# The mixer's output projection as seven quarter products, in a one-core encoder layer on Trainium2

## The reference, cut to what matters

```python
def hybrid_mixer(x, w_in, ..., w_out):
    ...
    return jnp.concatenate([att, hm.reshape(B, S, ML_WIDTH)], axis=-1) @ w_out

def memory_cross_attention(x, mem, w_cq, w_ck, w_cv, w_co):
    q = (x @ w_cq).reshape(B, S, MEM_HEADS, MEM_HD)
    k = (mem @ w_ck).reshape(B, -1, MEM_HEADS, MEM_HD)
    v = (mem @ w_cv).reshape(B, -1, MEM_HEADS, MEM_HD)
    ...

def reference(x, mem, ...):
    mix = hybrid_mixer(h, ...)
    h = layer_norm(DEEPNORM_ALPHA * h + mix, ln1_g[l], ln1_b[l])
    ca = memory_cross_attention(h, mem, ...)
    h = layer_norm(DEEPNORM_ALPHA * h + ca, ln2_g[l], ln2_b[l])
    ff = moe_ffn(h, ...)          # 32 experts, w_gu and w_down
    h = layer_norm(DEEPNORM_ALPHA * h + ff, ln3_g[l], ln3_b[l])
```

## Time and profile before

| | |
|---|---|
| median of 3 runs | 1160.19 us (1160.15 to 1160.58) |
| the profiled execution: its time | 1160.38 us |
| its span (first to last instruction) | 1158.4 us |
| mean granted TensorE clock over the span | 0.965 |
| busy: PE, DVE, ACT, POOL | 92%, 33%, 15%, 6% |
| HBM read | 443.84 MB |

### The profile page before, as it was taken

One profiled execution on the slowest core, in us unless ns is written; L12 is line 12 of the kernel. 1 busy time (PEld: TensorE's weight loads), 2 busy tenths in 40 slices (PEclk: granted clock), 3 DMA queues, 4 the chain that ended last, 5 costly groups with the idle time before them and its releaser, 6 DMA issues.

```text
span 1158.4 us, 20097 instructions
## 1 busy us (share of the span) xinstructions
PE 1070.6 (92%) x8036; PEld 469.1 (40%) x8037; DVE 378.1 (33%) x1230; ACT 168.5 (15%) x380; POOL 64.8 (6%) x40
## 2 busy tenths in 40 slices
PE   9999999998999669999976669999989989998997
PEld 8668649653333213333322223333323333332333
DVE  1716545254333113333311113333323313332323
ACT  1123211211111001111100001111111111111112
POOL 0520451000000000000000000000000000000000
PEclk9999999999999979999998889999998999999999
DMA  9984246959999999999999999999999999999996
GB/s 329 374 287 146 74 145 255 409 198 411 427 435 432 431 431 431 429 434 432 432 431 431 433 429 434 432 431 432 430 432 431 433 430 428 432 429 432 430 423 250
DMA packets 36670, 445.33 MB, mean 384 GB/s; under 512 B 3936, under 2 KB 5216, under 8 KB 21696
## 3 DMA queue, kind: packets, MB, share of 16 engines
q1 hardware_dynamic: 33888, 439.85, 90.3%
q10 hardware_dynamic: 2752, 5.04, 1.3%
HBM read 443.84 MB, written 1.05 MB: 384 GB/s over the span
## 4 chain that ended last, share of the span: by engine, by line
PE 72%; DMA 23%; another core or an unknown queue 2%; DVE 2%; ACT 1%; issue 0%; SPq 0%; DVEq 0%
PE bank L923 23%; PE bank L948 13%; DMA ring<-in_w_down 11%; DMA ring<-in_w_gu 11%; PE bank L899 6%; PE bank L600 6%; PE bank L617 5%; PE bank L886 3%; PE bank L819 2%; PE bank L756 2%; PE bank L698 2%; PE bank L892 1%; PE bank L930 1%; PE bank L936 1%; PE bank L941 1%
## 5 line engine op out<-in xcount | busy, mean ns | idle before, releaser
L923 PE MATMUL bank<-ring,wk 128*32 128x512 f32 x3072 | 371.1, 634 | 64.7 <-DMA ring<-in_w_gu 64.7
L923 PEld LDWEIGHTS bank<-ring,wk 128*32 128x32 f32 x3072 | 103.9, 116 | 304.2 <-issue 266.4
L948 PE MATMUL bank<-ring,wk 128*32 128x512 f32 x1632 | 205.5, 601 | 7.4 <-DMA ring<-in_w_down 7.3
L1829 DVE TENSOR_SCALAR wk<-bank 128x256 f32<-128x256 f32 x51 | 21.6, 424 | 536.1 <-PE bank L923 536.1
L899 PE MATMUL bank<-wk 64*128 64x512 f32 x416 | 103.3, 615 | 2.9 <-ACT wk L1329 2.9
L948 PEld LDWEIGHTS bank<-ring,wk 128*32 128x32 f32 x1632 | 63.4, 110 | 76.9 <-issue 48.9
L1315 ACT ACTIVATE wk<-wk 128x256 f32<-128x256 f32 x51 | 21.2, 416 | 455.2 <-DVE wk L1829 455.2
L600 PE MATMUL bank<-ring 128*128 128x256 f32 x320 | 70.4, 380 | 0.0
L899 PEld LDWEIGHTS bank<-wk 64*128 64x128 f32 x416 | 35.8, 186 | 71.5 <-issue 64.1
L600 PEld LDWEIGHTS bank<-ring 128*128 128x128 f32 x320 | 60.3, 190 | 8.4 <-issue 0.3
L886 PE MATMUL bank<-res,wk 128*32 128x256 f32 x832 | 56.5, 389 | 0.0
(11 more groups left out here) (333 smaller groups left out, 860.7 us busy)
## 6 DMA issues: line engine op xcount, KB each, us to landing
ring<-in_w_gu SPq DMA_DIRECT2D x55, 4096.0 KB, 34.7
ring<-in_w_down SPq DMA_DIRECT2D x27, 4096.0 KB, 38.3
ring<-in_w_gu SPq DMA_DIRECT2D x18, 2048.0 KB, 14.5
ring<-in_w_down SPq DMA_DIRECT2D x9, 2048.0 KB, 11.9
ring<-in_w_in SPq DMA_DIRECT2D x4, 2048.0 KB, 24.5
ring<-in_w_ck SPq DMA_DIRECT2D x2, 2048.0 KB, 22.0
ring<-in_w_cv SPq DMA_DIRECT2D x2, 2048.0 KB, 13.8
ring<-in_w_out SPq DMA_DIRECT2D x2, 2048.0 KB, 15.2
```

The source lines that it names most:

```text
L923: ins = mm(hidden(bank, g), rows[:, kk, c, :], half_columns(w[:, kk, :], g), start=False, stop=2 * c + kk == KT - 1, skip_group_check=True)
L948: ins = mm(strip(7, 2 * d + b), actT[:, b, 2 * c + gg, :], wd[:, gg, b, 512 * d:512 * d + 512], start=c == 0 and gg == 0 and b == 1, stop= ...
```

## The change

It does six things.

1. `wo0` and `wo1` become seven quarter products into banks 4, 5 and 6 (X, Y, Z), four matmuls each. Three of them add to a bank in place. They wait on `wo_sums` (input sums ready) and `wo_added` (a bank has been read).
2. DVE makes the sums: `wo_t1` and `wo_t3` before the copy of `hmT`; `wo_s1` to `wo_s4`, `wo_t2` and `wo_t4` between the products. Three of the weight sums are written over quarters of the weights.
3. DVE adds the products to `res` as they come: seven additions in place of four, each with one PSUM bank, and takes the statistics in halves between them.
4. `cq_t1` and `cq_t3` move on DVE from before the projection to between the projection's fifth and sixth product's additions.
5. POOL's sums for `cv` start on `wo_sums` 3 in place of `mixer_done`.
6. `wo_t1` uses the place of `lnp`, so the load of the first LayerNorm's parameters (ACT's queue) is issued after the fourth product; both `wo` slots are released to SP after the seventh.

```diff
@@ SP
             elif piece == "co0":
                 eng.wait_ge(co_half, 1)
+            elif piece in ("wo0", "wo1"):
+                eng.wait_ge(wo_product, 7)
@@ POOL
-            pool.wait_ge(mixer_done, 1)
+            pool.wait_ge(wo_sums, 3)
             pool.wait_ge(memT_landed, 16)
@@ PE
-            project("wo0", tT, order=(4, 5, 6, 7, 0, 1, 2, 3), late="pv")
-            project("wo1", tT)
+            landed("wo0")
+            landed("wo1")
+            X, Y, Z = psum[4], psum[5], psum[6]
+            quarter_product(X, mixed[0][0], wo_quarter[0][0]).then_inc(wo_product, 1)
+            wait_taken(pe, "pv")
+            quarter_product(Y, mixed[0][1], wo_quarter[1][0]).then_inc(wo_product, 1)
+            pe.wait_ge(wo_sums, 1)
+            quarter_product(Z, wo_s1, wo_t1).then_inc(wo_product, 1)
+            pe.wait_ge(wo_sums, 2)
+            pe.wait_ge(wo_added, 1)
+            quarter_product(X, wo_s2, wo_t2, fresh=False).then_inc(wo_product, 1)
+            pe.wait_ge(wo_sums, 3)
+            pe.wait_ge(wo_added, 3)
+            quarter_product(Z, wo_s4, wo_quarter[1][1], fresh=False).then_inc(wo_product, 1)
+            pe.wait_ge(wo_added, 4)
+            quarter_product(X, wo_s3, wo_t3, fresh=False).then_inc(wo_product, 1)
+            pe.wait_ge(wo_sums, 4)
+            quarter_product(Y, mixed[1][1], wo_t4).then_inc(wo_product, 1)
@@ ACT
-            act_e.dma_start(lnp, ln_p[0:1].to_broadcast([P, 2 * D])).then_inc(ln_landed[0], 16)
...
+            act_e.wait_ge(wo_product, 4)
+            act_e.dma_start(lnp, ln_p[0:1].to_broadcast([P, 2 * D])).then_inc(ln_landed[0], 16)
             rstd(0, 0)
@@ DVE, before the copy of hmT
+            link(v.tensor_tensor(wo_t1, wo_quarter[0][1], wo_quarter[0][0], ALU.subtract))
+            v.tensor_tensor(wo_t3, wo_quarter[1][1], wo_quarter[0][1], ALU.subtract)
@@ DVE, after it
+            v.tensor_tensor(wo_s1, mixed[1][0], mixed[1][1], ALU.add).then_inc(wo_sums, 1)
+            dve.wait_ge(wo_sums, 1)
+            v.tensor_tensor(wo_s2, wo_s1, mixed[0][0], ALU.subtract)
+            dve.wait_ge(wo_product, 1)
+            add_to_residual(0, 0, X).then_inc(wo_added, 1)
+            v.tensor_tensor(wo_t2, wo_quarter[1][1], wo_t1, ALU.subtract).then_inc(wo_sums, 1)
+            dve.wait_ge(wo_sums, 2)
+            v.tensor_tensor(wo_s4, mixed[0][1], wo_s2, ALU.subtract)
+            v.tensor_tensor(wo_s3, mixed[0][0], mixed[1][0], ALU.subtract).then_inc(wo_sums, 1)
...
```

More of the change, by code:

```diff
@@ L174, in layer_program @@
         queries = [[cqT[:, 4 - 4 * i:8 - 4 * i, t * P:t * P + P] for i in range(2)] for t in range(TT)]
+        wo_s1, wo_s2, wo_s3, wo_s4 = (S10[:, half + 512 * i:half + 512 * i + 512].rearrange("p (k t) -> p k t", k=KT // 2) for i in range(4))
+        wo_t1 = lnp.rearrange("p (k n) -> p k n", k=KT // 2)
+        mixed = [[tT[:, 4 - 4 * h:8 - 4 * h, t * P:t * P + P] for h in range(2)] for t in range(TT)]
+        wo_quarter = [[ring[:, s * SLOT + half - half * h:s * SLOT + SLOT - half * h].rearrange("p (k n) -> p k n", k=KT // 2)
+                       for s in (front_slot("wo0")[0], front_slot("wo1")[0])] for h in range(2)]
+        wo_t2, wo_t3, wo_t4 = wo_quarter[0][0], wo_quarter[0][1], wo_quarter[1][0]
         values = [[memV[:, t, 512 * i:512 * i + 512] for i in range(2)] for t in range(TT)]
@@ L604, in project_T, with project @@
                 return ins
-            def project(u, lhs, order=range(KT), late=None, between=None):
+            def project(u, lhs, between=None):
                 banks = open_unit(u)
@@ L611, in project @@
                 for t in range(TT):
-                    for n, k in enumerate(order):
-                        if between and t == 1 and n == 5:
+                    for k in range(KT):
+                        if between and t == 1 and k == 5:
                             between()
-                        if late and t == 0 and n == KT // 2:
-                            wait_taken(pe, late)
-                        ins = mm(banks[t][:], lhs[:, k, t * P:(t + 1) * P], w[:, k, :], start=n == 0, stop=n == KT - 1)
+                        ins = mm(banks[t][:], lhs[:, k, t * P:(t + 1) * P], w[:, k, :], start=k == 0, stop=k == KT - 1)
                 close_unit(u, ins)
@@ L694, in _, with quarter_product @@
             project_T("ck1", memT_sb)
-            def quarter_product(bank, rows, cols):
+            def quarter_product(bank, rows, cols, fresh=True):
                 for k in range(KT // 2):
-                    ins = mm(bank[:], rows[:, k, :], cols[:, k, :], start=k == 0, stop=k == KT // 2 - 1)
+                    ins = mm(bank[:], rows[:, k, :], cols[:, k, :], start=fresh and k == 0, stop=k == KT // 2 - 1, skip_group_check=True)
                 return ins
@@ L1551, in _ @@
                 v.tensor_copy(tT[:, 4 + 2 * i:6 + 2 * i, :], unit_banks("hmT")[i][:].rearrange("p (m t) -> p m t", m=2)).then_inc(taken["hmT"], 1)
[L1553 to L1559, removed]
             def statistics(t):
@@ L1585, in take_transposed, with add_product @@
                 v.tensor_copy(tT[:, 0:4, t * P:(t + 1) * P], unit_banks(u)[0][:].rearrange("p (k t) -> p k t", k=4)).then_inc(taken[u], 1)
-            dve.wait_ge(x_landed, 16)
[L1588 to L1595, removed]
+            def add_product(t, i, bank):
+                c = slice(512 * i, 512 * i + 512)
+                return v.tensor_tensor(res[:, t, c], res[:, t, c], bank[:], ALU.add)
@@ new lines, in half_statistics @@
+            def half_statistics(t, i):
+                return v.bn_stats(lst[:, t, i, :], res[:, t, 512 * i:512 * i + 512])
+            X, Y, Z = psum[4], psum[5], psum[6]
+            dve.wait_ge(x_landed, 16)
+            wait_taken(dve, "hmT")
+            wait_taken(dve, "pv")
+            v.tensor_tensor(wo_s1, mixed[1][0], mixed[1][1], ALU.add).then_inc(wo_sums, 1)
+            dve.wait_ge(wo_sums, 1)
+            v.tensor_tensor(wo_s2, wo_s1, mixed[0][0], ALU.subtract)
+            dve.wait_ge(wo_product, 1)
@@ new lines, in _ @@
+            add_to_residual(0, 0, X).then_inc(wo_added, 1)
[3 more added lines that the diff above has]
+            v.tensor_tensor(wo_s3, mixed[0][0], mixed[1][0], ALU.subtract).then_inc(wo_sums, 1)
+            dve.wait_ge(wo_product, 2)
+            dve.wait_ge(wo_added, 1)
+            add_product(0, 0, Y).then_inc(wo_added, 1)
+            v.tensor_tensor(wo_t4, wo_quarter[1][0], wo_t2, ALU.subtract).then_inc(wo_sums, 1)
@@ new lines, in _ @@
+            dve.wait_ge(wo_product, 3)
+            add_to_residual(1, 1, Z).then_inc(wo_added, 1)
+            dve.wait_ge(wo_product, 4)
+            add_to_residual(0, 1, X).then_inc(wo_added, 1)
+            dve.wait_ge(wo_added, 4)
+            half_statistics(0, 0)
+            dve.wait_ge(wo_product, 5)
+            add_product(0, 1, Z).then_inc(wo_added, 1)
+            dve.wait_ge(wo_added, 5)
+            link(half_statistics(0, 1))
+            v.bn_aggr(lag[:, 0, :], lst[:, 0].rearrange("p c s -> p (c s)")).then_inc(var_ready, 1)
@@ new lines, in _ @@
+            for piece in ("cq0", "cq1"):
+                s, n = front_slot(piece)
+                dve.wait_ge(slot_landed[s], 16 * n)
+            link(v.tensor_tensor(cq_t1, cq_quarter[0][1], cq_quarter[0][0], ALU.subtract))
+            v.tensor_tensor(cq_t3, cq_quarter[1][1], cq_quarter[0][1], ALU.subtract)
+            dve.wait_ge(wo_product, 6)
+            add_product(1, 1, X).then_inc(wo_added, 1)
+            add_to_residual(1, 0, X).then_inc(wo_added, 1)
+            dve.wait_ge(wo_added, 7)
```

16 lines of the change are left out of this document (12 added, 4 removed).

## The result

The changed kernel takes 1163.95 us (median of 12 runs, 1161.64 to 1166.81); the kernel before took 1160.17 us in the runs beside it (12 runs, 1158.59 to 1162.91). The ratio is 1.0032, with an interval of 1.0024 to 1.0041: slower by about 3.8 us, where I forecast no change and a range up to 1163.6.

The account below looks back on a forecast made before the run. The expert part is bound by its loads, which stream once the PE-bound front part ends. A gain of 3.45 us less 0.3, 2.05 and 1.2 gives -0.1, taken as 0: 1160.38 plus 0, so 1160.4 us; range 1158.2 to 1163.6.

Parts of the forecast that it names:

- Part 1: Output projection on PE: seven products instead of eight take 24.0 us, everything behind comes 3.45 us earlier, the whole possible gain.
- Part 2: DVE's sums between the projection's products: PE's waits between the seven products priced at 0, with 1.9 us of cover.
- Part 3: POOL's sums for cv start 7.6 us later; the late start alone costs 0, with 4.4 us or more of cover.
- Part 4: DVE and POOL exclude each other at SBUF during cv and normalisation; PE loses 0.3, 2.05 and 1.2 us.
- the sum: Start of the queries' products: 3.45 - 0.3 - 2.05 - 1.2 = -0.1 us, taken as nothing.
- Part 5: Smaller edits: moved loads of LayerNorm parameters and co1 cost 0; half statistics beside POOL 0, upper bound 3.6 us.
- The step that failed: Tile 1's normalisation on DVE meets two POOL combining additions, about 1.15 us each; ready about 175.7, PE loses 1.2 us.
- The term that was missing: PE's clock in the front part is granted in full; nothing to be gained or lost there unless PE pauses; no price.
- Rival A: Tile 1's normalisation: POOL wins the ties, two more additions, 2.4 us, 1162.8; with statistics held up to 1165.2; chance 0.25.
- The link to the end: SP's expert loads start when the front part ends, so a shift of the queries' products moves the end one for one.

Follow-up runs that it names:

- the late-POOL run: The kernel before, with POOL's sums started only after DVE's two large sums and 30 tiny memsets on DVE; 1160.37 us, ratio 0.9998.
- the two runs with late sums: The changed kernel with cq_t1 and cq_t3 made behind the transposes, among the queries' products: 1157.39 us; the same with POOL's combining additions held until both tiles are normalised: 1157.01.
- the run with the memsets: The changed kernel with a tiny POOL memset ahead of each of four of its combining additions; 1160.17 us, ratio 0.9999 to the kernel before.
- the matmuls in the gap: The changed kernel with three more 128x512 matmuls on PE between the two tiles' transposes; 1163.86 us, ratio 1.0028 to the kernel before.
- the sums back: The changed kernel with cq_t1 and cq_t3 back at their old place behind pv, ahead of wo_s1; 1164.06 us, ratio 1.0023 to the kernel before.
- the hold: The changed kernel with POOL's six combining additions waiting until both token tiles are normalised; 1160.70 us, ratio 1.0003 to the kernel before.

## Why the prediction was wrong

**Right, to a few tenths** (after subtracting the start's 0.85). Part 1: nine products run in 31.17 us without a gap. Part 2: no wait between the seven products. Part 3: the late start costs 0, shown alone by the late-POOL run. Part 4, the meetings: announcements reckoned at 151.4, 161.1, 166.6 and 167.8 came at 151.6, 161.4, 166.9 and 168.1; POOL's second sum at 6.45, its seventh at 5.48, `cq_t1` at 4.88, the Newton step at 4.34 (forecast: near 6.4, 5.5, 4.7, over 4). PE's waits ahead of `cvB1` are 0.56 and 1.68, together 2.24 where 2.35 stood in the sum. The last `cv` product ends at 174.05 against 173.5, since the third announcement came 0.3 us late and the two products behind it took 7.13 us in place of 6.86: 0.7 us of the gain are left there and not 1.1. It changed nothing, for the second tile came later still. Tile 0 is normalised at 169.8 against 169.5.

Part 5: the statistic beside POOL took 0.69 us and held nobody, while POOL was in its second sum, whose 6.45 us are `wo_t4`'s doing alone (142.15, the end of `wo_t4`, and 4.36 us are 146.51, where the sum ends). By the Trainium skill (SBUF — State Buffer, Who interferes with whom), where a VectorE instruction with at most one SBUF input does not contend, the term was to be 0: the trace agrees. The loads cost nothing, as the two runs with late sums show, which keep them where the change put them.

**The step that failed** is the last one of Part 4: "two stand in its way if DVE is granted the port in the near ties that follow". Four stood in its way, besides the one that its first half met. Tile 1 was ready at 179.11, less 0.85 is 178.3, not 175.7: 2.55 us, of which 0.3 are tile 0's and the rest are two additions. From tile 0 to tile 1 it took 8.45 us; with POOL held it took 3.36, so 5.1 us were waiting, in five meetings. The forecast had 6.2 us, as in the run with the memsets, and there they are three meetings. By its own words it would be fewer: 169.5, 3.35 of work and two additions of 1.15 make 175.2, not 175.7, so the meeting of the first half is in the time and not in the count. I took the ties from one row in which POOL had nothing queued, where no tie could be seen, and chose the cheap side: no row in hand favoured either, and I gave them 0.58 and 0.25. In the three profiles that have the two near ties (the changed kernel, the matmuls in the gap, the sums back) POOL goes first all six times.

**The term that was missing** is the clock. I wrote that nothing was to be lost "unless PE pauses", forecast pauses, and did not price them. A pause of 3.39 us was followed by 0.50 of the clock and cost 1.5 us (with the sums back the same pause was followed by 0.58 and cost 1.7; pauses of 1.68 and 1.09 us were followed by a clock of 1.00). For the sum: the forecast was 0.1 us slower, and 0.1 + 2.55 + 1.5 = 4.15, where the front stretch is 4.1 longer. That the clock's 1.5 us reach the end no run shows by itself. Rival A was the right case, but at 1162.8 it was short by that clock, and the range that it set, to 1163.6, missed 1163.95.

**The link to the end** was right. In eight of the ten profiles the third expert's first load goes out 60.1 to 60.3 us behind the queries' products; in the other two, before and the matmuls in the gap, which have the low clock ahead of the routing, it is 61.6 and 61.7. The time of each profiled execution less the start of that load is 897.0 to 898.7 us in all ten. In the medians, front stretches of +4.1, +0.4, 0.0 and -3.4 us end at +3.8, -0.3, -0.1 and -3.2 to -3.5. The loosest are the run with the sums back, +2.7 against +3.6, and the hold, -0.7 against +0.15, both within the intervals. How often a kernel has the low clock ahead of the routing is not known, so up to 1.7 us of any difference at the end may be that.

## What to carry to other kernels

When work is moved between DVE and POOL, list the instructions of either that read SBUF (DVE's with two such inputs) by the time at which they are asked for, and count meetings, not busy time: each costs up to the whole length of the other's instruction, so long instructions belong away from chains of tiny ones that somebody waits for. Follow the chain of waits over the engine that makes the last input, too: the two sums that were moved here stood with 8.1 us in DVE's chain to the second tile, and putting them behind it gave the whole gain. Where two queues arrive within some tenths of a microsecond, price both orders and forecast the dear one as readily as the cheap one; an extra instruction of 0.1 us may change which of them meet, and a semaphore that lets the critical engine finish removes the question (4.8 us in the front stretch here). And where a pause of PE like the one here (3.39 us) is forecast, price what runs behind it at half clock too.

## What the runs showed of the hardware

- DVE and POOL exclude each other where both read SBUF, DVE with two inputs: a DVE instruction of 0.16 us took 4.34 us behind a POOL sum, and ended 0.02 us after it.
- The starts in the trace do not tell who gets the port when they are 0.02 us apart: DVE's rows at 174.05 and 176.74 start ahead of POOL's at 174.07 and 176.76, and DVE is the one held both times. With equal starts, at 172.71 and 174.24 in the run with the memsets, DVE is not held.
- DVE instructions with one SBUF input were not held beside POOL's sums: a statistic of 128x512 took 0.69 us, an addition with a PSUM bank 0.67 to 0.69.
- POOL memsets of 0.10 us, one ahead of each of four additions, changed the order enough to be worth 3.8 us in the end.
- The granted clock was 0.50 after a pause of PE of 3.39 us (0.58 in a second case) and 1.00 after pauses of 0.56, 1.68 and 1.09 us.
